# Two transformer blocks on one core: the MLP in four parts, the embedding's product shared between two norms

## The chip, the cores and the metric

The program runs on one core of one Trainium2 chip. The metric is the device time of one execution in microseconds, median of several runs. The core's engines are TensorE (matmuls; PE in the profile), VectorE (DVE), ScalarE (ACT), GpSimd (POOL) and SyncE (SP), whose queue issues the loads of weights.

## The reference

A first block (a gated delta rule mixer, then sliding-window attention) and a second block over 512 tokens of width 1024. The change touches the second block from the mixer's output product on, of which this is the code:

```python
mix = jnp.concatenate([y_pool, y_sb], axis=-1) @ w_out[i]
h = h + rms_norm_2(mix, g_mix_post[i])

m = rms_norm_2(h, g_mlp_pre[i]) @ w_up[i]          # 1024 -> 4096
m = jnp.square(jax.nn.relu(m)) @ w_down[i]         # 4096 -> 1024
h = h + rms_norm_2(m, g_mlp_post[i])

gate = jax.nn.sigmoid(h @ w_ple_gate[i])           # 1024 -> 1024
e = rms_norm_2(p[i] @ w_ple_proj[i], g_ple[i])     # 256 -> 1024
h = h + gate * e
```

All of it is in float32.

## The kernel before

**Layout.** Activations lie transposed: channels on the 128 partitions, the 512 tokens along the free axis, so a tensor of width 1024 is eight tiles of 128x512. A product's output of 128 channels is a "group", made in one of the PSUM banks.

**Products.** Each float32 operand is split in a high and a low part, and a product of one 128x128 piece of weights is three matmuls (high x high, high x low, low x high), made by `mm3` through line L736. One such triple is a "step". Weights come in blocks of eight pieces (128x1024, 512 KB). SyncE loads a block into one of four raw buffers, ScalarE makes its high part (L1223), VectorE its low part (L1819); `Pace` says at which point of the program each block is split: two blocks ahead as a rule (`open`), or a burst (`ahead`). `block_order` lists the blocks in the order of use.

**Order.** Every engine has a program of its own, and all follow one common script, `follow`. `gemm` is a generator whose `walk` yields the events OPEN, MM, LATE, CLOSE and STEP. With `wide` = 3 the first three groups go side by side, a piece of each in turn, so that a product can start while its inputs still arrive. CLOSE is where VectorE and ScalarE drain a group. `take(g, n)` advances a generator by n steps, `do` runs a named part of each engine that has one. Six banks (`WIDE`) are used in rotation.

**Norms.** The squares of eight tiles (ScalarE, `square`) are added up on VectorE (`accumulate`; L2214 for the first, L2217 for the others) into `sqa`; `rstd` sums over partitions by two float32 matmuls with a matrix of ones (`sqa`, and the last square in `sqt`), and ScalarE takes Ln (L1533) and Exp (L1547) into `rb`.

**Around the change.** After the mix product `rstd(3)` gives the factor and `post(0)` runs through eight pieces: VectorE scales the drained `mo` (L2418), the residual is added into `h` (piece 0 on VectorE, L2422, pieces 1 to 7 on GpSimd, L2583), ScalarE writes the high part of the next product's input `xm` (L1764), VectorE the low part (L2411; L2409 in `post(1)`). The semaphore `hv` stands for piece 0, `h[2]` and `h[3]` for the others. The squares of the new `h` are made and added behind that (`stats_h`), with 21 steps of the up product in between, and then `rstd(4)`.

The MLP goes in two halves of the inner width, each an up product of 16 groups and a down product of eight groups of 16 pieces. An up group is drained by relu times factor (VectorE, L1971, into `sqt`), square (ScalarE, L1275), high part (ScalarE, L1279) and low part (VectorE, L1974) into `xr`. The first down product is drained by ScalarE (L1289), the second by an add on VectorE (L1982). `begin_p` loads and splits the embedding's input between the halves.

Behind the MLP stands `ple`, the embedding's product: eight groups of two steps, each drained twice by ScalarE (L1788 a copy, L1793 a square into `pf`) and followed by a matmul of that square with the ones matrix. `rstd(5)` stands after the fourth. `post(1)` then feeds the gate product, `rstd(6)` scales the embedding (L2228), and each gate group ends with sigmoid (L1296), a product and an add (L1990, L1995) and its store.

Of the kernel before, what the change touches and what calls it, by code (L numbers as in the profile page):

```python
# [63 lines left out]

def block_order():
# [70 lines left out]
def walk(groups, wide=0, skew=0):  # L136
# [4 lines left out]
    if wide:  # L141
# [10 lines left out]
        for n in range(wide):  # L152
            yield CLOSE, n, groups[n][-1]
            yield STEP,
    for n in range(wide, len(groups)):
        blocks = groups[n]
        for at, i in enumerate(blocks):
            yield OPEN, n, i, at == 0
            for kk in range(8):
                k = 8 * at + kk  # L160
                yield MM, n, i, kk, k, k == 0, k == 8 * len(blocks) - 1
                yield STEP,
        yield CLOSE, n, blocks[-1]
        yield STEP,
# [63 lines left out]
def weave(g, order, parts, beside):  # L228
# [8 lines left out]
    for name in parts:  # L237
# [12 lines left out]
         "stick0": 12, "stick1": 14, "ple": 8}  # L250
# [10 lines left out]
def follow(p):  # L261
# [137 lines left out]
    for _ in range(3):  # L399
        next(up)  # L400
    drain(up)
    for half in range(2):
        if half:
            drain(gemm("up", single_groups("wu", 16, 16), 0, 1))
            do("begin_p")
        drain(gemm("down", [[("wd", 16 * half + 2 * n), ("wd", 16 * half + 2 * n + 1)] for n in range(8)], 0, half))

    ple = part("ple")
    for _ in range(4):
# [13 lines left out]
class Memory:  # L423
# [123 lines left out]

    def gain(self, key, i):
        return self.gcol[key][:, i:i + 1]
# [10 lines left out]
    def pieces(self, key):  # L560
# [4 lines left out]
        if key in ("ao", "bo", "down"):  # L565
            return [(x[:, k, :], x[:, 16 + k, :]) for k in range(16)]
# [7 lines left out]
class Signals:  # L574


    def __init__(self, nc, ctx):
        def new(name):
# [34 lines left out]
        self.h, self.hv = [new(f"h{n}") for n in range(4)], new("h_first_piece")  # L613
# [25 lines left out]
        self.d0, self.d1 = new("down_first"), new("down_second")  # L639
        self.phi, self.plo = new("p_hi"), new("p_lo")  # L640
        self.pe_p, self.pe_e, self.pe_s, self.pe_sum, self.pe_v = (
            new(n) for n in ("ple_pe", "ple_kept", "ple_sq", "ple_sum", "ple_scaled"))
# [80 lines left out]
def tensor_program(e, m, s):  # L723
# [24 lines left out]
    def await_piece(name, k, a):  # L748
# [18 lines left out]
        elif name == "down":  # L767
            e.wait_ge(s.hidlo, 16 * a + k + 1)
# [3 lines left out]
    def drained(name, n, a):  # L772
# [18 lines left out]
        if name == "up":  # L791
            return [(s.relu, 16 * a + n + 1)]
        if name == "down":
            return [((s.d0, s.d1)[a], n + 1)]
# [3 lines left out]
    def gemm(name, groups, wide=0, a=None, skew=0):  # L798
        X, bank = m.pieces(name), {}
        for what, *at in walk(groups, wide, skew):  # L800
# [178 lines left out]
    def rstd(r):  # L979
        if r == 6:  # L980
            return
# [191 lines left out]
    def ple():  # L1173
        def total(f):
            if f == 0:
                cleared(3)
            e.wait_ge(s.pe_s, f + 1)
            mm(m.banks[3][:], m.ones, m.pf[:, f % 2, :], f == 0, f == 7).then_inc(s.pe_sum, 1)

        for f in range(8):  # L1180
            half, n = f // 4, f % 4
            i = BLOCK["wp", half]
            wh = m.wh[:, i % N_SPLIT, :].rearrange("p (n k m) -> p n k m", n=4, k=2)
            wl = m.wl[:, i % N_SPLIT, :].rearrange("p (n k m) -> p n k m", n=4, k=2)
            b = ring.next()
            cleared(b)
            if n == 0:
                e.wait_ge(s.wlo, i + 1)
            if f == 0:
                e.wait_ge(s.plo, 2)  # L1190
            for k in range(2):
                ins = mm3(m.banks[b][:], wh[:, n, k, :], wl[:, n, k, :], m.xp[:, k, :], m.xp[:, 2 + k, :], k == 0, k == 1)
            ins.then_inc(s.wused if n == 3 else s.pe_p, 1)
            clear[b] = [(s.pe_e, f + 1), (s.pe_s, f + 1)]
            if f:
                total(f - 1)
            yield
        total(7)
# [4 lines left out]
def scalar_program(e, m, s):  # L1203
# [22 lines left out]
    def gemm(name, groups, wide=0, a=None, skew=0):  # L1226
        bank = {}
        for what, *at in walk(groups, wide, skew):
# [42 lines left out]
    def evac_up(n, bank, i, half):  # L1271
        f = m.sqt[:, n % 2, :]
        at = 16 * half + n + 1
# [3 lines left out]
        if n == 0:  # L1277
            e.wait_ge(s.wused, (BLOCK["wd", 15] if half else BLOCK["wco", 7]) + 1)
        e.activation(m.XR[:, n, :], f, ACT.Copy).then_inc(s.hidhi, 1)  # L1279

    def evac_down(n, bank, i, half):
        if half:
            square(4, n)
            return
        e.wait_ge(s.wused, i + 1)
        if n == 0:
            e.wait_ge(s.hv, 1)
            e.wait_ge(s.h[2], 7)
        e.activation(m.mo[:, n, :], bank[:], ACT.Copy).then_inc(s.d0, 1)  # L1289

    def evac_gate(n, bank, i, a):
        e.wait_ge(s.wused, i + 1)
        if n == 0:
            e.wait_ge(s.hv, 2)
            e.wait_ge(s.h[3], 7)
# [205 lines left out]
    def square(r, n, tile=None):  # L1501
# [15 lines left out]
        elif r == 3 and n == 0:  # L1517
            e.wait_ge(s.hv, 1)
        elif r == 3:
            e.wait_ge(s.h[2], n)  # L1520
        elif r == 4:
            e.wait_ge(s.d1, n + 1)
# [5 lines left out]
    def rstd(r):  # L1528
        if r == 6:
            e.wait_ge(s.pe_sum, 8)  # L1530
# [225 lines left out]
    def post(at):  # L1756
        for n in range(8):
            if n == 0:
                e.wait_ge(s.hv, at + 1)
                e.wait_ge(s.wused, (BLOCK["wd", 31] if at else BLOCK["wco", 7]) + 1)  # L1760
            else:
                e.wait_ge(s.h[2 + at], n)
            scale = 1.0 if at else m.gain("g_mlp_pre", n)
            e.activation(m.xm[:, n, :], m.H[:, n, :], ACT.Copy, scale=scale).then_inc(s.shi, 1)  # L1764
            if n == 1:
                split(pace.ahead(4))
# [8 lines left out]
    def ple():  # L1775
# [1049 lines left out]
```

## Time and profile before

| | us |
|---|---|
| runs | 1678.0, 1679.5, 1684.57; median 1679.5 |
| profiled execution | 1678.48, its span in the profile 1676.7 |
| TensorE busy | 1580.9 (94%), mean granted clock 0.984 |
| VectorE busy | 865.4 (52%) |
| ScalarE busy | 745.0 (44%) |
| GpSimd busy | 264.9 (16%) |
| chain that ended last | 79% TensorE, 8% VectorE, 7% ScalarE |

The span runs from the first instruction to the last; the profiled execution's own time has 1.8 us around it. Busy shares are means over all stages. The granted clock is TensorE's, as a share of full speed (2.4 GHz); its lower level, 0.50, is 1.2 GHz.

### The profile page before, as it was taken

How to read it: one execution, taken by the hardware profiler on the slowest of the kernel's cores; microseconds unless marked ns; L12 is line 12 of the kernel's file. 1: busy time of each engine (PE TensorE's matmuls, PEld its weight loads, DVE VectorE, ACT ScalarE, POOL GpSimd, SP SyncE). 2: the span in 40 equal slices, each digit the busy share in tenths (PEclk: the TensorE clock that was granted, in tenths of full speed). 3: DMA queues.
4: the chain of work that ended last, by engine and by line, in shares of the span. 5: the costliest groups of instructions: out<-in, count | busy, mean ns of one | idle time of the engine just before them, and what ended most of it. 6: DMA issues, size and time to landing. Idle time of an engine off the chain costs nothing.

```text
span 1676.7 us, 20632 instructions
## 1 busy us (share of the span) xinstructions
PE 1580.9 (94%) x7700; PEld 1238.5 (74%) x7700; DVE 865.4 (52%) x1596; ACT 745.0 (44%) x1293; POOL 264.9 (16%) x465
## 2 busy tenths in 40 slices
PE   7789999998889999999998999999989999999988
PEld 5577888887777876777775787666667888888866
DVE  4667666766654455555555435444365422444346
ACT  4443454345443255656666323555535322343243
POOL 1033324332222000322222200000020000000010
PEclk9799999999999999999999999999989999999999
DMA  4121211111113323122221132111122233222321
GB/s 176 63 76 39 63 64 63 54 50 44 45 51 105 101 90 113 64 76 74 72 76 60 61 100 83 53 56 49 50 70 88 95 106 101 88 90 99 101 75 51
DMA packets 40163, 127.22 MB, mean 76 GB/s; under 512 B 4576, under 2 KB 9104, under 8 KB 40064
## 3 DMA queue, kind: packets, MB, share of 16 engines
q1 hardware_dynamic: 38112, 121.65, 22.3%
q0 software_dynamic: 1040, 3.27, 0.6%
q8 instruction: 62, 1.02, 0.2%
q10 hardware_dynamic: 912, 0.99, 0.2%
q14 instruction: 37, 0.30, 0.1%
HBM read 122.69 MB, written 2.15 MB: 74 GB/s over the span
## 4 chain that ended last, share of the span: by engine, by line
PE 79%; DVE 8%; ACT 7%; issue 3%; POOL 2%; DMA 1%; SPq 0%; ACTq 0%; DVEq 0%; POOLq 0%
PE ps L736 77%; ACT L L1627 3%; DVE wl L1819 2%; DVE L L2295 1%; PE ps L1065 1%; PE ps L861 1%; ACT wh L1223 1%; POOL h L2583 1%; DVE qkv L1855 1%; DMA wraw<-in_wa 1%; DVE qb L1904 1%; POOL L L2568 1%; ACT L L1579 0%; DVE mo L2418 0%; DVE U L2148 0%
## 5 line engine op out<-in xcount | busy, mean ns | idle before, releaser
L736 PE MATMUL ps<-xr,wh 128*128 128x512 f32 x2752 | 902.2, 409 | 17.7 <-DVE wl L1819 15.3
L736 PEld LDWEIGHTS ps<-xr,wh 128*128 128x128 f32 x2752 | 504.7, 190 | 145.9 <-issue 40.8
L736 PE MATMUL ps<-xr,wl 128*128 128x512 f32 x1376 | 543.2, 395 | 0.0
L1819 DVE TENSOR_TENSOR wl<-wraw,wh 128x1024 fp32r<-128x1024 f32 x214 | 261.1, 1233 | 181.9 <-ACT wh L1223 180.6
L736 PEld LDWEIGHTS ps<-xr,wl 128*128 128x128 f32 x1376 | 261.0, 190 | 57.7
L1223 ACT ACTIVATE wh<-wraw 128x1024 fp32r<-128x1024 f32 x214 | 220.6, 1048 | 34.1 <-PE ps L736 30.4
L736 PE MATMUL ps<-xm,wh 128*128 128x512 f32 x640 | 202.5, 398 | 11.4 <-DVE xm L2411 7.1
L736 PEld LDWEIGHTS ps<-xm,wh 128*128 128x128 f32 x640 | 121.5, 191 | 42.5 <-issue 9.4
L2568 POOL TENSOR_SCALAR L<-L,m 128x256 f32<-128x256 f32 (+1 forms) x128 | 80.7, 655 | 313.8 <-DVE m L2310 313.8
L736 PE MATMUL ps<-xm,wl 128*128 128x512 f32 x320 | 126.1, 394 | 0.0
L2583 POOL TENSOR_TENSOR h<-h,mo 128x512 f32<-128x512 f32 x14 | 20.5, 1462 | 598.0 <-DVE mo L2418 598.0
L1855 DVE SCALAR_TENSOR_TENSOR qkv<-cin,gains,qkv 128x512 f32<-128x512 f32 x96 | 73.7, 769 | 4.0 <-ACT qkv L1251 3.0
L1627 ACT ACTIVATE L<-L,m 128x256 f32<-128x256 f32 (+1 forms) x128 | 59.9, 469 | 28.3 <-DVE m L2301 28.3
L736 PEld LDWEIGHTS ps<-xm,wl 128*128 128x128 f32 x320 | 61.2, 191 | 13.1
L1275 ACT ACTIVATE sqt<-sqt 128x512 f32<-128x512 f32 x32 | 20.2, 632 | 92.8 <-DVE sqt L1971 92.8
L2295 DVE CUSTOM_DVE_ANT_0 L<-ps,bias,sinks 128x256 f32<-128x256 f32 (+1 forms) x128 | 51.1, 443 | 19.8 <-PE ps L736 19.8
L1525 ACT ACTIVATE sqt<-h 128x512 f32<-128x512 f32 x24 | 15.0, 630 | 101.1 <-DVE h L1884 54.6
L2536 POOL TENSOR_TENSOR masks<-nb,uc 128x60 f32<-128x60 f32 (+14 forms) x120 | 45.0, 375 | 79.1 <-DVE nb L2115 63.0
L1251 ACT ACTIVATE qkv<-cin,gains 128x512 f32<-128x512 f32 x32 | 23.0, 722 | 66.2 <-DVE cin L1869 66.2
L1647 ACT ACTIVATE pT<-ps 128x512 f32<-128x512 f32 x32 | 19.2, 599 | 71.9 <-PE ps L1065 71.8
L2538 POOL TENSOR_TENSOR uc<-uc,masks 128x60 f32<-128x60 f32 (+14 forms) x120 | 43.4, 362 | 9.4
L1974 DVE TENSOR_TENSOR xr<-sqt,xr 128x512 fp32r<-128x512 f32 x32 | 22.2, 692 | 43.6 <-ACT xr L1279 43.6
(257 smaller groups left out, 1801.5 us busy)
## 6 DMA issues: line engine op xcount, KB each, us to landing
wraw<-in_wa SPq DMA_DIRECT2D x48, 512.0 KB, 3.8
wraw<-in_wb SPq DMA_DIRECT2D x32, 512.0 KB, 3.8
wraw<-in_wu SPq DMA_DIRECT2D x32, 512.0 KB, 3.7
wraw<-in_wd SPq DMA_DIRECT2D x32, 512.0 KB, 3.7
wraw<-in_wao SPq DMA_DIRECT2D x16, 512.0 KB, 3.7
wraw<-in_wbo SPq DMA_DIRECT2D x16, 512.0 KB, 3.8
wraw<-in_wc SPq DMA_DIRECT2D x16, 512.0 KB, 3.7
bias<-rel_rows SPq DMA_DIRECT2D x16, 256.0 KB, 4.0
```

The lines of the kernel that those rows point to most:

```text
L736: return e.matmul(out, w, x, start=start, stop=stop, skip_group_check=True)
L1223: e.activation(m.wh[:, i % N_SPLIT, :], m.raw[:, i % N_RAW, :], ACT.Copy).then_inc(s.whi, 1)
L1251: e.activation(m.qkv[:, h % 2, n, :], m.cin[:, b, 3:515], ACT.Copy, scale=m.convw[:, 3, ch:ch + 1]).then_inc(s.conv0, 1)
L1627: e.activation(x, x, ACT.Exp, bias=m.nmx[:, c, u:u + 1], accum_out=m.den[:, c, u:u + 1]).then_inc(s.ex, 1)
L1819: e.tensor_tensor(m.wl[:, i % N_SPLIT, :], m.raw[:, i % N_RAW, :], m.wh[:, i % N_SPLIT, :].bitcast(F), ALU.subtract).then_inc(s.wlo, 1)
L1855: e.scalar_tensor_tensor(out=dst, in0=m.cin[:, c % 2, w:w + 512], scalar=m.convw[:, w, ch:ch + 1], in1=dst, op0=ALU.mult, op1=ALU.add).the ...
L1974: e.tensor_tensor(m.XR[:, 16 + n, :], f, m.XR[:, n, :].bitcast(F), ALU.subtract).then_inc(s.hidlo, 1)
L2295: e.tensor_tensor_reduce(out=m.L[:, c, ee, n, lo:], in0=m.banks[4 + ee][:, 256 * (n % 2) + lo:256 * (n % 2) + 256], in1=m.bias[:, c, ee, lo:],
L2536: did(e.tensor_tensor(part, nb[:, :, r + 1:], m.uc[:, :, r:r + 1].to_broadcast([128, 4, w]), ALU.mult))
L2538: did(e.tensor_tensor(m.uc[:, :, r + 1:], m.uc[:, :, r + 1:], part, ALU.add))
L2568: e.tensor_scalar(x, x, m.den[:, c, 2 * n + ee:2 * n + ee + 1], 1.0, ALU.mult, ALU.mult).then_inc(s.pr, 1)
L2583: e.tensor_tensor(m.H[:, n, :], m.H[:, n, :], m.mo[:, n, :], ALU.add).then_inc(s.h[2 + at], 1)
```

## The change

- The MLP goes in four parts of 1024 inner channels: up of eight groups, down of eight groups of eight pieces, four times. The first down product is drained by ScalarE, the other three are added to it by VectorE. The hidden tiles' low parts are made one group later than before, behind the next group's relu, and `up_end` makes the last.
- The embedding's product is cut in two halves of four groups; one half stands at the norm after the mix (one step of it ahead of `rstd(3)`, seven behind), the other at the norm after the MLP. The blocks `wp` move accordingly in the order of weights, and `begin_p` moves into the mix product.
- The squares of the embedding are no longer summed by eight matmuls: ScalarE squares the kept tiles later (four behind the first up product, four in the gate product), VectorE adds them up, and one matmul with the ones matrix remains.
- All residual adds are on VectorE, each followed by the next piece's scaling; GpSimd's `post` is gone.
- In the up product of part 0 and in the gate product the three wide groups start one piece apart (`skew` = 1) and two more groups are made before any is drained (`hold` = 2). The sums of the squares of `h` are added in behind the 24 wide steps, and `rstd(4)` and `rstd(6)` stand ten steps into the held groups.

```diff
+def up_groups(a):
+    return [[("wu", 8 * a + n)] for n in range(8)]
+def down_groups(a):
+    return [[("wd", 16 * (a // 2) + 2 * n + a % 2)] for n in range(8)]
...
-    for half in range(2):
-        out += [("wu", 16 * half + b) for b in range(16)]
-        out += [("wd", 16 * half + b) for b in range(16)]
-    out += [("wp", b) for b in range(2)]
+    out += [("wp", 0)]
+    for a in range(4):
+        out += [b for g in up_groups(a) + down_groups(a) for b in g]
+    out += [("wp", 1)]
...
-def walk(groups, wide=0, skew=0):
+def walk(groups, wide=0, skew=0, hold=0):
...
         yield LATE,
-        for n in range(wide):
-            yield CLOSE, n, groups[n][-1]
-            yield STEP,
+    done = list(range(wide))
     for n in range(wide, len(groups)):
+        if done and n == wide + hold:
+            yield from close(groups, done)
+            done = []
...
-        yield CLOSE, n, blocks[-1]
+        done.append(n)
+        if n >= wide + hold:
+            yield from close(groups, done)
+            done = []
+    yield from close(groups, done)
...
+    drain(take(mix, 24))
+    do("begin_p")
     drain(mix)
-    do("rstd", 3)
-    do("post", 0)
-    up = gemm("up", single_groups("wu", 16), 3, 0)
-    for n in range(8):
-        do("stats_h", n)
-        for _ in range(3 if n < 7 else 0):
-            next(up)
-    do("rstd", 4)
...
+    def normed(r, at):
+        ple = part("ple", at)
+        post = part("post", at)
         next(ple)
-    do("rstd", 5)
-    drain(ple)
-    do("post", 1)
-    gate = gemm("gate", single_groups("wg", 8), 3)
+        do("rstd", r)
+        drain(take(ple, 3))
+        for _ in range(2):
+            next(post)
+            drain(take(ple, 2))
+        drain(ple)
+        drain(post)
+
+    normed(3, 0)
+    for a in range(4):
+        up = gemm("up", up_groups(a), *((0, a) if a else (3, a, 1, 2)))
+        if a == 0:
+            drain(take(up, 24))
+            for n in range(8):
+                if n == 4:
+                    next(up)
+                do("stats_h", n)
+            drain(take(up, 9))
+            do("rstd", 4)
+        drain(up)
+        do("up_end", a)
+        if a == 0:
+            for f in range(4):
+                do("square_e", f)
+        drain(gemm("down", down_groups(a), 0, a))
+
+    normed(5, 1)
+    gate = gemm("gate", single_groups("wg", 8), 3, None, 1, 2)
+    drain(take(gate, 24))
+    for f in range(4, 8):
+        do("square_e", f)
+    drain(take(gate, 9))
     do("rstd", 6)
     drain(gate)
...
     def rstd(r):
         if r == 6:
+            cleared(3)
+            e.wait_ge(s.pe_acc, 7)
+            mm(m.banks[3][:], m.ones, m.esum).then_inc(s.pe_sum, 1)
             return
...
-            if f:
-                total(f - 1)
-            yield
-        total(7)
...
+    def square_e(f):
+        e.wait_ge(s.pe_e, f + 1)
+        if f >= 3:
+            e.wait_ge(s.pe_acc, f - 2)
+        elif f:
+            e.wait_ge(s.plo, 2)
+        e.activation(m.pf[:, f % 2, :] if f else m.esum, m.e[:, f, :], ACT.Square).then_inc(s.pe_s, 1)
...
+        if n:
+            hid_low(n - 1, a)
+    def hid_low(n, a):
+        e.wait_ge(s.hidhi, 8 * a + n + 1)
+        e.tensor_tensor(m.XR[:, 8 + n, :], m.sqt[:, n % 2, :], m.XR[:, n, :].bitcast(F),
+                        ALU.subtract).then_inc(s.hidlo, 1)
...
-        e.tensor_tensor(m.mo[:, n, :], bank[:], m.mo[:, n, :], ALU.add).then_inc(s.d1, 1)
-        accumulate(4, n)
+        e.wait_ge(s.down[a - 1], n + 1)
+        e.tensor_tensor(m.mo[:, n, :], bank[:], m.mo[:, n, :], ALU.add).then_inc(s.down[a], 1)
+        if a == 3:
+            accumulate(4, n)
...
+        scaled(0)
+        for n in range(8):
+            e.wait_ge(s.post, 8 * at + n + 1)
+            e.tensor_tensor(m.H[:, n, :], m.H[:, n, :], m.mo[:, n, :], ALU.add).then_inc(s.h[2 + at], 1)
+            if n < 7:
+                scaled(n + 1)
+            low(n)
+            if n in (1, 5):
+                split(pace.ahead(3 if n == 1 else 4))
+            yield
...
-    def post(at):
-        for n in range(1, 8):
-            e.wait_ge(s.post, 8 * at + n + 1)
-            e.tensor_tensor(m.H[:, n, :], m.H[:, n, :], m.mo[:, n, :], ALU.add).then_inc(s.h[2 + at], 1)
```

## Rows read from the trace of the kernel before

**Rows 1.** The page, busy time of TensorE: us, share of the span, instructions.
```profile
PE 1580.9 (94%) x7700; PEld 1238.5 (74%) x7700; DVE 865.4 (52%) x1596; ACT 745.0 (44%) x1293; POOL 264.9 (16%) x465
```

**Rows 2.** TensorE's waits, 1180 to the end: releaser, us in total, times, longest.
```profile
PE ps L736 <- DVE xm L2411: 7.1, 4, 5.6
PE ps L736 <- DVE xm L2409: 3.9, 5, 1.4
PE ps L736 <- DVE sqa L2217: 3.8, 1, 3.8
```

**Rows 3.** The drains of the first down half: duration min/median/max, first and last start.
```profile
L1289 ACT ACTIVATE mo<-ps x8: 598/598/598, 1351.3 to 1427.4; 128x512 f32<-128x512 f32 x8
```

**Rows 4.** Timeline of TensorE, first norm: start, us, instruction, [idle before, releaser].
```profile
1232.80 1.12 PE L736 MATMUL ps<-sqt,k 128*128 128x512 f32 x2
...
1239.52 0.77 PE L736 MATMUL ps<-xm,wh 128*128 128x512 f32 x1 [5.60 <-DVE xm L2411]
...
1263.97 1.10 PE L736 MATMUL ps<-sqa,k 128*128 128x512 f32 x2 [3.84 <-DVE sqa L2217]
```

**Rows 5.** Timelines of VectorE and of ScalarE, first norm.
```profile
1235.34 0.75 DVE L2418 SCALAR_TENSOR_TENSOR mo<-mo,gains,rb 128x512 f32<-128x512 f32 x1 [5.35 <-ACT rb L1547]
1236.12 0.69 DVE L2422 TENSOR_TENSOR h<-h,mo 128x512 f32<-128x512 f32 x1
...
1249.08 1.78 DVE L2418 SCALAR_TENSOR_TENSOR mo<-mo,gains,rb 128x512 f32<-128x512 f32 x1
...
1254.02 1.77 DVE L2418 SCALAR_TENSOR_TENSOR mo<-mo,gains,rb 128x512 f32<-128x512 f32 x1
...
1259.15 4.67 DVE L2217 TENSOR_TENSOR sqa<-sqa,sqt 128x512 f32<-128x512 f32 x6
...
1238.86 0.72 ACT L1764 ACTIVATE xm<-h,gains 128x512 fp32r<-128x512 f32 x1 [1.29 <-POOL h L2583]
```

**Rows 6.** Timeline of GpSimd, first norm.
```profile
1248.57 1.74 POOL L2583 TENSOR_TENSOR h<-h,mo 128x512 f32<-128x512 f32 x1 [1.29 <-DVE mo L2418]
```

**Rows 7.** Windows: length, busy of PE, PEld, DVE, ACT, POOL, granted clock, DMA share, GB/s.
```profile
120.00:124.00 4.00, 1.18 (x8) 0.78 (x8) 0.00 (x0) 3.34 (x5) 0.00 (x0) 1.00 0.01 2
484.00:488.00 4.00, 2.00 (x10) 1.78 (x11) 3.59 (x5) 4.00 (x8) 1.23 (x1) 0.86 0.00 0
1240.00:1248.00 8.00, 7.39 (x18) 5.20 (x17) 7.20 (x7) 2.88 (x4) 2.99 (x2) 0.50 0.39 131
1480.00:1520.00 40.00, 40.00 (x178) 33.10 (x178) 20.35 (x25) 17.49 (x24) 0.00 (x0) 1.00 0.28 92
```

**Rows 8.** Timeline of TensorE, second norm: sums by the ones matrix.
```profile
1609.55 1.02 PE L736 MATMUL ps<-pf,k 128*128 128x512 f32 x2
1610.41 1.02 PE L736 MATMUL ps<-sqa,k 128*128 128x512 f32 x2
```

**Rows 9.** Timelines of VectorE and ScalarE, second norm.
```profile
1601.51 0.69 DVE L1982 TENSOR_TENSOR mo<-ps,mo 128x512 f32<-128x512 f32 x1 [6.12 <-PE ps L736]
...
1602.29 0.63 ACT L1525 ACTIVATE sqt<-mo 128x512 f32<-128x512 f32 x1 [8.35 <-DVE mo L1982]
...
1640.70 0.69 DVE L2409 TENSOR_TENSOR xm<-h,xm 128x512 fp32r<-128x512 f32 x1
```

**Rows 10.** Timelines of VectorE and of ScalarE, gate product.
```profile
1642.01 5.39 DVE L2228 SCALAR_TENSOR_TENSOR xreg<-xreg,gains,rb 128x512 f32<-128x512 f32 x8 [0.62 <-ACT rb L1547]
1647.32 1.22 DVE L1819 TENSOR_TENSOR wl<-wraw,wh 128x1024 fp32r<-128x1024 f32 x1
1648.45 0.69 DVE L1990 TENSOR_TENSOR mo<-mo,xreg 128x512 f32<-128x512 f32 x1
...
1649.78 0.68 DVE L1990 TENSOR_TENSOR mo<-mo,xreg 128x512 f32<-128x512 f32 x1
...
1643.72 1.06 ACT L1223 ACTIVATE wh<-wraw 128x1024 fp32r<-128x1024 f32 x1 [1.81 <-PE ps L736]
...
1672.22 0.60 ACT L1296 ACTIVATE mo<-ps 128x512 f32<-128x512 f32 x1 [4.84 <-PE ps L736]
```

More of the change, by code:

```diff
@@ L791, in drained, with gemm @@
         if name == "up":
-            return [(s.relu, 16 * a + n + 1)]
+            return [(s.relu, 8 * a + n + 1)]
         if name == "down":
-            return [((s.d0, s.d1)[a], n + 1)]
+            return [(s.down[a], n + 1)]
         return [(s.gs, n + 1)]
     @part
-    def gemm(name, groups, wide=0, a=None, skew=0):
+    def gemm(name, groups, wide=0, a=None, skew=0, hold=0):
         X, bank = m.pieces(name), {}
-        for what, *at in walk(groups, wide, skew):
+        for what, *at in walk(groups, wide, skew, hold):
             if what == OPEN:
@@ L1225, in gemm @@
     @part
-    def gemm(name, groups, wide=0, a=None, skew=0):
+    def gemm(name, groups, wide=0, a=None, skew=0, hold=0):
         bank = {}
-        for what, *at in walk(groups, wide, skew):
+        for what, *at in walk(groups, wide, skew, hold):
             if what == OPEN:
@@ L1774, in ple @@
     @part
-    def ple():
-        for f in range(8):
-            half, n = f // 4, f % 4
+    def ple(half):
+        split(pace.open())
+        for n in range(4):
+            f = 4 * half + n
             b = ring.next()
-            if n == 0:
-                split(pace.open())
-                if half == 0:
-                    e.wait_ge(s.wused, BLOCK["wd", 31] + 1)
+            yield
             if n == 3:
@@ L1822, in gemm @@
     @part
-    def gemm(name, groups, wide=0, a=None, skew=0):
+    def gemm(name, groups, wide=0, a=None, skew=0, hold=0):
         bank = {}
-        for what, *at in walk(groups, wide, skew):
+        for what, *at in walk(groups, wide, skew, hold):
             if what == OPEN:
@@ L2435, in ple, with square_e @@
     @part
-    def ple():
-        for f in range(8):
+    def ple(half):
+        split(pace.open())
+        for n in range(4):
             ring.next()
-            if f % 4 == 0:
-                split(pace.open())
-            if f % 4 == 3:
-                pace.finish()
             yield
+            yield
+        pace.finish()
+    @part
+    def square_e(f):
+        if f:
+            e.wait_ge(s.pe_s, f + 1)
+            if f > 1:
+                e.wait_ge(s.pe_acc, f - 1)
+            e.tensor_tensor(m.esum, m.esum, m.pf[:, f % 2, :], ALU.add).then_inc(s.pe_acc, 1)
     follow(p)
@@ L2455, in gemm @@
     @part
-    def gemm(name, groups, wide=0, a=None, skew=0):
-        for what, *_ in walk(groups, wide, skew):
+    def gemm(name, groups, wide=0, a=None, skew=0, hold=0):
+        for what, *_ in walk(groups, wide, skew, hold):
             if what == STEP:
@@ L2616, in gemm @@
     @part
-    def gemm(name, groups, wide=0, a=None, skew=0):
-        for what, *at in walk(groups, wide, skew):
+    def gemm(name, groups, wide=0, a=None, skew=0, hold=0):
+        for what, *at in walk(groups, wide, skew, hold):
             if what == OPEN:
@@ L2673, in post, with ple @@
     def post(at):
-        split(pace.ahead(4))
+        for n in range(8):
+            if n in (1, 5):
+                split(pace.ahead(3 if n == 1 else 4))
+            yield
     @part
-    def ple():
-        for f in range(8):
-            if f % 4 == 0:
-                split(pace.open())
-            if f % 4 == 3:
-                pace.finish()
-            yield
+    def ple(half):
+        split(pace.open())
+        yield from idle(8)
+        pace.finish()
     @part
```

143 lines of the change are left out of this document (56 added, 87 removed).

## The prediction

> **What bounds it now.** The page comes first: TensorE is busy for 94% of the span [rows 1], so time can only come out of its gaps, its slow stretches, or work taken from it. Next I read its waits over the part that the diff touches, from the mix product to the end [rows 2]: 14.8 us, all of it beside the two norms that feed the up product (7.1 and 3.8) and the gate product (3.9); inside the MLP there is none. Then its speed where nothing holds it: the eight drains of the first down half start over 76.1 us, 16 steps of three matmuls apart, so a step (one 128x128 piece of weights, high and low parts) costs 76.1 / 7 / 16 = 0.68 us [rows 3]. Then, engine by engine, the norms.
>
> First norm. Statistics end, Ln and Exp follow, VectorE scales, adds, and feeds piece by piece [rows 5]. TensorE stands 5.60 us before its first up piece and 3.84 us before the second statistics, for which VectorE makes its adds only after the last piece [rows 4, 6]. The granted clock is 0.50 from 1240 to 1248, the lower of its two levels [rows 7]. From the second statistics 491 of the MLP's 512 steps are left; at 0.68 (0.6795 unrounded) they take 333.6 us, and TensorE starts them at 1265.7 and ends at 1601.5: another 2.2 us lost to the clock. The pieces come slowly because GpSimd adds seven of eight residual pieces: beside one of its 1.74 us adds VectorE's scaling takes 1.78 us in place of 0.75 [rows 5, 6].
>
> Second norm. The embedding's eight products (two steps each) run first, each with a sum by the 128x128 ones matrix: such a sum takes 0.86 us (start to start) [rows 8]. The last gate piece is written from 1640.70 on, 39.2 us behind the last down drain at 1601.51 [rows 9].
>
> **The change, part by part.** All in time of the trace of before.
>
> Statistics to first scaling. Before the statistics' two sums TensorE now runs one embedding step, 0.68 us. From the second sum's start to the first scaling it was 1235.34 - 1232.80 = 2.54 us, and stays so; hence s, the start of the first scaling, is 1235.34 + 0.68 = 1236.02. ScalarE's weight split (1.05 [rows 10]) for the embedding's opening falls into the time before that sum ends. The other seven steps (4.8 us) run from 1234.3 to 1239.1, under the chain.
>
> Pieces, on VectorE alone. Per piece: add 0.69, ScalarE's pass 0.72, the low part, and in the shadow of that pass the next scaling. With 0.02 us from engine to engine and a scaling's pitch of (5.39 - 0.75) / 7 = 0.66 [rows 10], the period is 0.69 + 0.02 + 0.72 + 0.02 + 0.66 = 2.11 us; in the second norm, with ScalarE at 0.63 and a subtraction of pitch 0.61 [rows 9, 10], 1.97. In before, scalings two pieces apart start 4.94 us apart (1249.08, 1254.02), 2.47 a piece [rows 5]. The first low part starts at s + 0.78 + 1.45 = s + 2.23 (second norm s + 2.14). Two weight splits stand in the row: each waits for ScalarE's 1.05 and takes 1.13, less 0.66 overlapped, 1.5 us each. The last low part is done at s + 2.23 + 14.8 + 3.0 + 0.75 = s + 20.8 = 1256.8. The first is done at 1239.0, as TensorE ends the embedding: the 5.6 us gap goes.
>
> Skew and hold. The three wide groups start one piece apart, and two more follow before any is drained, so from the last piece TensorE has 6 + 10 = 16 steps, 10.9 us, to 1267.7. The next statistics (4.67 us for six adds [rows 5], the copy, two or three weight splits of 1.2) end about 7 us behind the last piece, near 1264: the 3.84 goes. Two sums, 1.72, and 512 - 34 = 478 steps, 324.8 us, follow: the last down group ends at **1594.2**, against 1601.5. First term: **7.3 us**.
>
> MLP in four parts. The count of matmuls stays. VectorE gets 16 more drains of 0.69, ScalarE none; VectorE was busy about half the time in the MLP's busiest window (20.35 of 40 us [rows 7]), so nothing. New are three more handovers from up to down. The first down group needs the last hidden tile only at its eighth step, 4.8 us in; that tile's chain is relu 0.69, square 0.63, copy 0.63, subtraction 0.69 and hops, 2.8 us: 2 us to spare. Five held tiles leave behind the norm's factor; with relu of the next tile ahead of this one's subtraction both engines need about 1.4 a tile, 7 us, and the sixth group has a free bank, the seventh the first drained: no wait. The embedding's squares (0.6) and adds (0.72) stand behind the last hidden tile and ahead of a split wanted two groups (10.9 us) later: hidden. The input p and its split move from the MLP into the mix product; its DMA, behind y on GpSimd's queue, lands before ScalarE asks, and on SyncE's queue one block of the embedding's weights only takes the place of another block of the same size: nothing.
>
> Second norm, counted from the old 1601.5. One step to 1602.2, first sum to 1603.0; the square of the last down tile ends at 1602.92 [rows 9], in time. Second sum from 1603.0, s = 1605.6; embedding done at 1608.6. The last piece is done at s + 2.14 + 13.8 + 3.0 + 0.69 = s + 19.6 = 1625.2. 46 steps are left, 31.3 us, and one sum, 0.86: TensorE ends at 1657.4. In before it ends at 1672.2, where the last sigmoid starts [rows 10]. Second term: **14.8 us**; 6.0 of it is the seven sums of 0.86 that VectorE and ScalarE now make between other work. One place is tight. Counted from the start of the sum for the embedding, its factor is there after 2.5 us (sum, Ln, Exp); VectorE then scales eight tiles (5.31), drains five held groups (1.33 each [rows 10]: 6.65) and splits the last weights (1.2): 15.8 with hops. TensorE wants these weights after the sum's 0.86, six steps and two groups of eight (15.0): 15.8 too. 0 to 0.5 us, taken as 0.1. The sum itself is a new wait of TensorE, with group five of the gate queued behind it; its last term is added near 1628, and TensorE gets there at 1625.2 + 10.9 = 1636.1.
>
> The clock. In the skewed start TensorE has one step for the first piece and two for the second, and the first split delays the third: gaps of 1.3 and 2.2 us, 1.4 us of work in 5. What follows is not in the trace of before. Nearest rows: with 1.18 us of work in 4 the clock stayed at 1.00 (120 to 124); with 2.00 in 4 it fell (0.86 from 484 on); behind 5.60 and 3.84 us of standing it fell [rows 4, 7]. The one stretch at the lower level lasted 8.5 us (1239.5 to 1248), the other, from the 2.2 us it lost, about 4.4. Below it costs nothing; above, 8.5 us at half speed lose 4.3, less 1.5 of gaps that hold it: 2.8 in each norm, 5.6 in all. I take 1.5, one fall in two norms. The Trainium skill, "TensorE: Matmul & The Clock Gate", section "A second HAM failure mode: psum-queue depth-cycling", says that short idling between groups of matmuls can make the clock swing between its levels; by that rule both norms would see it, which is rival (a). The row of 120 to 124 speaks against it here, that of 484 for it.
>
> Sum: 7.3 + 14.8 - 0.1 - 1.5 = 20.5 us. The profiled execution took 1678.5, so 1658.0; it lies 1.0 below the median of the runs, 1679.5. Forecast **1659**.
>
> **Rivals.**
> (a) The clock falls in both norms and stays low for as long as the longest stretch: 4.1 beyond what I took, 1663. For: gaps of 1.3 to 2.2 in both. Against: six steps in a row come behind them.
> (b) VectorE's row is no faster than before, because scaling and add do not overlap behind each other's signals: the period stays near 2.47. 7 x (0.36 + 0.50) = 6.0 us: 1665. For: three operations and two handovers in each piece. Against: VectorE's long times stand only beside GpSimd [rows 5, 6].
> (c) Handovers wait: the last two hidden tiles go through one behind the other and behind a split, 2 x 2.75 + 1.2 = 6.7 against 4.8 at four places: 7.7 us, 1667. Against: both engines are idle most of an up group.
> (d) The other side: the thinner start keeps TensorE at half clock. A step costs 0.55 us more there (7.39 us for 18 matmuls [rows 7], 1.23 against 0.68). It decides from (22.0 + 3) / 0.55 = 46 steps on; if all 24 wide and 10 held steps of both norms run so, 68 steps cost 37 less 3 us of gaps: 1657.5 + 34 = 1692. Against: no row shows more than 8.5 us of it.
> (e) The change does not do what it says only if the chain through the norms was not the limit; the waits name its members one by one [rows 2].
>
> **How the numbers follow.** Forecast case 0.62, (a) 0.14, (b) 0.11, (c) 0.07, (d) 0.03, something cheaper than every bound (no fall at all, smaller hops) 0.03. The forecast case alone runs from 1655.5 (no clock loss, hops 1 us less) to 1662. With (a) and most of (b) the range is 1654.5 to 1665.5; outside are (c), (d) and the rest. A difference of 0.5% (8.4 us) is about what a measurement can tell: all but (d) are faster than 1671.
>
> **What would show it.** No idle of TensorE over 2.5 us in either norm; first scaling near 1236.0, last low part of the first norm near 1256.8; period 2.1; the second statistics waited for by nobody; last down tile near 1594; one ones-sum before the gate's factor; from there to the last piece 24 us. A third piece that starts at clock 0.50, a TensorE wait on the hidden low part (the eighth step of a down group), or on the weights of the last gate group would show it wrong.

## The result

The changed kernel takes 1660.5 us (median of 4 runs, 1657.0 to 1662.2) against 1681.1 for the kernel before (4 runs, one more than the three known at the forecast): ratio 0.9874, 95% interval 0.9847 to 0.9902. Forecast were 1659 and a range of 1654.5 to 1665.5. The profiled execution took 1661.3, its span 1659.5.

The spans differ by 17.2 us, less than the 20.5 I had worked out, but not where the diff is. I compare one stretch, from the start of ScalarE's last square of the mix product to the start of the last gate sigmoid, cut at the start of the last down drain on VectorE:

| us | mix to last down drain | to the last sigmoid | stretch |
|---|---|---|---|
| before | 369.4 | 70.7 | 440.1 |
| changed | 362.8 | 56.5 | 419.3 |
| difference | 6.6 | 14.3 | **20.8** |
| predicted (7.3 and 14.8, less 1.6) | | | 20.5 |

The stretch begins at 1232.1 before and at 1235.7 in the changed kernel, though the change leaves what stands ahead of it, but for `begin_p` in the mix product, as it was. The mean granted clock of the spans, 0.984 and 0.981, makes 53 and 63 us at the lower level, of which the stretch itself has 13.7 and 3.4. Of the 3.6 us, 2.9 arise between 620 and 666 us, where only the changed kernel's trace has a fall (6.8 us, from 641 on); where the clock falls there differs from execution to execution. All experiments below are therefore read from the stretch of their one profile first, and from their runs second. A part of the stretch that an edit leaves alone comes out the same to 0.1 us, except where the clock differs inside it (0.3 us in the second part of e6, 0.85 in the first of e8).

TensorE's waits from 1180 on, changed kernel (who was waited for, us in total, times, longest):

```profile
PE ps L776 <- DVE xm L2445: 3.7, 3, 1.8
PE ps L776 <- DVE xm L2447: 3.0, 2, 1.9
PE ps L776 <- ACT am L1755: 1.1, 1, 1.1
```

They answer to [rows 2]: 14.8 us have become 6.7 (L2447 is the low part of the first norm, L2445 that of the second). The wait for the statistics (`sqa`) has gone. For the rest an estimate from these traces: waits for the embedding's squares and for a block of weights (1.5 us) are gone too, seven sums of 0.86 are gone (6.0), and TensorE works 3.4 us at the lower clock and not 11.3, which at half speed is 3.9. With the 8.1 us of waits that makes 19.5 of the 20.8.

Timeline of TensorE in the first norm, changed kernel (start, us, instruction, idle before it), against [rows 4]:

```profile
1237.06 1.02 PE L776 MATMUL ps<-sqt,k 128*128 128x512 f32 x2
...
1244.78 0.73 PE L776 MATMUL ps<-xm,wh 128*128 128x512 f32 x2 [1.12 <-DVE xm L2447]
...
1248.35 0.85 PE L776 MATMUL ps<-xm,wh 128*128 128x512 f32 x2 [1.91 <-DVE xm L2447]
...
1271.52 1.02 PE L776 MATMUL ps<-sqa,k 128*128 128x512 f32 x2
```

The second statistics start with no idle time ahead of them. The longest gap is 1.9 us where it was 5.6. VectorE, the same norm, against [rows 5]:

```profile
1239.50 0.75 DVE L2454 SCALAR_TENSOR_TENSOR mo<-mo,gains,rb 128x512 f32<-128x512 f32 x1 [0.51 <-ACT rb L1575]
1240.29 0.69 DVE L2460 TENSOR_TENSOR h<-h,mo 128x512 f32<-128x512 f32 x1
...
1248.21 0.68 DVE L2460 TENSOR_TENSOR h<-h,mo 128x512 f32<-128x512 f32 x1
...
1250.35 0.69 DVE L2460 TENSOR_TENSOR h<-h,mo 128x512 f32<-128x512 f32 x1
...
1254.93 1.23 DVE L1848 TENSOR_TENSOR wl<-wraw,wh 128x1024 fp32r<-128x1024 f32 x1 [0.20 <-ACT wh L1255]
...
1259.69 0.75 DVE L2447 SCALAR_TENSOR_TENSOR xm<-h,gains,xm 128x512 fp32r<-128x512 f32 x1 [0.79 <-ACT xm L1790]
```

From one residual add to the next 2.14 us (2.11 predicted); the first scaling starts 2.44 us behind the second sum (2.54), the last low part ends 20.94 behind the first scaling (20.8). The granted clock there (windows; columns as in [rows 7]):

```profile
1246.00:1248.00 2.00, 0.44 (x2) 0.01 (x1) 1.87 (x4) 0.72 (x1) 0.00 (x0) 1.00 0.40 84
1248.00:1250.00 2.00, 1.65 (x5) 1.31 (x6) 1.88 (x4) 0.72 (x1) 0.00 (x0) 0.70 0.44 178
1250.00:1252.00 2.00, 2.00 (x7) 1.51 (x6) 1.87 (x4) 0.73 (x1) 0.00 (x0) 0.50 0.00 0
1252.00:1254.00 2.00, 2.00 (x10) 1.66 (x9) 1.87 (x4) 0.78 (x2) 0.00 (x0) 0.95 0.00 0
```

Behind the gap it fell to 0.50 (1.2 GHz), for 3.4 us. It happened in one norm of two. The Trainium skill, "TensorE: Matmul & The Clock Gate", section "A second HAM failure mode: psum-queue depth-cycling", describes a clock that swings between its levels where TensorE idles shortly and often between groups of matmuls; here the trace agrees in the first norm (one fall, behind gaps of 1.1 and 1.9 us) and not in the second (none, behind 0.9 and 1.8).

The second norm on VectorE, and the first piece on ScalarE, against [rows 8 to 10]:

```profile
1598.53 0.69 DVE L2018 TENSOR_TENSOR mo<-ps,mo 128x512 f32<-128x512 f32 x1 [1.81 <-PE ps L776]
...
1602.55 0.75 DVE L2454 SCALAR_TENSOR_TENSOR mo<-mo,gains,rb 128x512 f32<-128x512 f32 x1 [0.40 <-ACT rb L1575]
...
1621.70 0.69 DVE L2445 TENSOR_TENSOR xm<-h,xm 128x512 fp32r<-128x512 f32 x1 [0.70 <-ACT xm L1790]
...
1635.35 5.39 DVE L2264 SCALAR_TENSOR_TENSOR xreg<-xreg,gains,rb 128x512 f32<-128x512 f32 x8 [6.06 <-ACT rb L1575]
...
1647.50 1.22 DVE L1848 TENSOR_TENSOR wl<-wraw,wh 128x1024 fp32r<-128x1024 f32 x1
...
1604.12 0.63 ACT L1790 ACTIVATE xm<-h 128x512 fp32r<-128x512 f32 x1 [0.29 <-DVE h L2460]
```

The first piece of the kernel before, where the last down drain starts at 1601.51:

```profile
1621.42 1.15 ACT L1764 ACTIVATE xm<-h 128x512 fp32r<-128x512 f32 x2
```

So ScalarE writes the first piece 5.6 us behind the last down drain, 19.9 before, and that is 14.3 us, as much as the whole second part gained. Behind it the last piece comes another 1.7 us sooner, and 1.8 us more follow the last piece.

TensorE, the late factor's sum by the ones matrix (`k`), inside the fifth gate group, with no idle time ahead of it (33 gate steps come before it, nine of them of the held groups and not ten; ahead of `rstd(4)` it is 34 up steps):

```profile
1632.84 1.02 PE L776 MATMUL ps<-xreg,k 128*128 128x512 f32 x2
```

The low part of the last piece starts 23.2 us behind the last down drain, 39.2 before. The last gate weights are ready at 1648.7, and TensorE does not wait for them.

### The profile page after: what moved, and what is told of

Read it like the earlier page. It is cut to its first block, busy times and chain, and to the rows that moved or that the text cites. A ratio compares the mean times of both kernels' runs of the same rounds, so it can differ in the third digit from the quotient of the medians.

```text
span 1659.5 us, 20679 instructions
## 1 busy us (share of the span) xinstructions
PE 1578.6 (95%) x7686; PEld 1240.5 (75%) x7686; DVE 875.4 (53%) x1633; ACT 746.9 (45%) x1293; POOL 244.3 (15%) x451
## 4 chain that ended last, share of the span: by engine, by line
PE 81%; DVE 7%; ACT 7%; issue 3%; POOL 1%; DMA 1%; SPq 0%; ACTq 0%; DVEq 0%; POOLq 0%
PE ps L776 79%; ACT L L1655 3%; DVE wl L1848 2%; DVE L L2331 1%; PE ps L1108 1%; PE ps L901 1%; ACT wh L1255 1%; DVE qkv L1884 1%; DMA wraw<-in_wa 1%; DVE qb L1933 1%; POOL L L2614 1%; ACT L L1607 0%; DVE h L2460 0%; DVE U L2184 0%; ACT xm L1790 0%
## 5 line engine op out<-in xcount | busy, mean ns | idle before, releaser
L2018 DVE TENSOR_TENSOR mo<-ps,mo 128x512 f32<-128x512 f32 x24 | 16.6, 692 | 66.9 <-PE ps L776 66.9
L1999 DVE SCALAR_TENSOR_TENSOR sqt<-ps,rb 128x512 f32<-128x512 f32 x32 | 22.0, 691 | 41.0 <-PE ps L776 36.0
```

Of the source, the lines that this page charges most:

```text
L1999: e.scalar_tensor_tensor(out=m.sqt[:, n % 2, :], in0=bank[:], scalar=0.0, in1=m.rb[:], op0=ALU.max, op1=ALU.mult).then_inc(s.relu, 1)
```

## The experiments

Columns: stretch and its two parts in us, from one profile; ratio of the runs to the kernel before with its 95% interval. The changed kernel stands in the first line. Each ratio is to runs of the kernel before made beside that version (their medians are 1680.2 to 1684.3), so ratios can be compared and medians only roughly. The expectations of e1 to e4 cut the stretch slightly differently (419.5 and 440.3 us for what is 419.3 and 440.1 here).

| | first part | second part | stretch | median of runs | ratio |
|---|---|---|---|---|---|
| changed | 362.8 | 56.5 | 419.3 | 1660.5 | 0.9874 (0.9847 to 0.9902) |
| e1 adds on GpSimd | 364.8 | 59.2 | 423.9 | 1662.8 | 0.9899 (0.9879 to 0.9919) |
| e2 no skew | 361.1 | 54.5 | 415.6 | 1656.0 | 0.9854 (0.9827 to 0.9881) |
| e3 sums back | 363.4 | 57.2 | 420.6 | 1660.6 | 0.9889 (0.9872 to 0.9906) |
| e5 embedding whole | 362.2 | 64.0 | 426.2 | 1667.2 | 0.9906 (0.9888 to 0.9923) |
| e10 the same, split in time | 362.4 | 58.0 | 420.4 | 1662.1 | 0.9875 (0.9857 to 0.9894) |
| e6 factor first | 363.9 | 56.8 | 420.7 | 1659.8 | 0.9862 (0.9845 to 0.9878) |
| e7 row cleared | 357.9 | 51.9 | 409.8 | 1648.5 | 0.9794 (0.9774 to 0.9814) |
| e11 e7, sums back | 360.7 | 55.4 | 416.1 | 1656.9 | 0.9847 (0.9828 to 0.9866) |
| before | 369.4 | 70.7 | 440.1 | 1681.1 | 1 |
| e4 before, four parts | 369.4 | 70.7 | 440.0 | 1683.6 | 1.0024 (1.0012 to 1.0035) |
| e8 before, one sum | 370.2 | 64.4 | 434.6 | 1676.7 | 0.9955 (0.9937 to 0.9973) |
| e9 before, adds on VectorE | 366.8 | 67.8 | 434.6 | 1676.2 | 0.9962 (0.9945 to 0.9978) |

**e1, the residual adds back on GpSimd** (changed kernel).

```diff
+            if n == 0:
                 e.tensor_tensor(m.H[:, n, :], m.H[:, n, :], m.mo[:, n, :], ALU.add).then_inc(s.h[2 + at], 1)
...
+    def post(at):                                   # GpSimd
+        for n in range(8):
+            if n:
+                e.wait_ge(s.h[2 + at], n)
+                e.wait_ge(s.post, 8 * at + n + 1)
+                e.tensor_tensor(m.H[:, n, :], m.H[:, n, :], m.mo[:, n, :], ALU.add).then_inc(s.h[2 + at], 1)
+            yield
```

> The changed kernel with residual adds 1 to 7 of both norms back on GpSimd. Stretch measured: end of the mix product to the start of the last gate sigmoid, 419.5 us in the changed kernel, 440.3 before. Theory (VectorE's row of add, scaling and low part sets the time to the last piece; GpSimd's adds slow it): a piece takes 2.47 again in place of 2.15 and 2.00, so 7 x 0.32 + 7 x 0.47 = 5.5 us more, 425. Rival (GpSimd takes work off VectorE and the add is hidden under ScalarE's pass): no change or less, 418 to 420.

Measured 423.9, 4.6 more against the theory's 5.5; the rival falls. VectorE, then GpSimd, in this run:

```profile
1246.18 0.74 DVE L2447 SCALAR_TENSOR_TENSOR xm<-h,gains,xm 128x512 fp32r<-128x512 f32 x1
1246.85 1.77 DVE L2454 SCALAR_TENSOR_TENSOR mo<-mo,gains,rb 128x512 f32<-128x512 f32 x1
1248.87 1.74 DVE L2447 SCALAR_TENSOR_TENSOR xm<-h,gains,xm 128x512 fp32r<-128x512 f32 x1 [0.24 <-ACT xm L1790]
...
1246.40 1.67 POOL L2632 TENSOR_TENSOR h<-h,mo 128x512 f32<-128x512 f32 x1 [1.35 <-DVE mo L2454]
```

The long operations of 1.77 and 1.74 us are back exactly beside GpSimd's adds. From the last low part to the last down drain it took 338.1 us, as in the changed kernel, and here the clock did not fall in the first norm: behind the last piece nothing is left of the changed kernel's fall.

**e2, no skew** (changed kernel): `(3, a, 1, 2)` becomes `(3, a, 0, 2)`, and the gate's skew 0 too.

> The changed kernel with skew 0 in the up product of part 0 and in the gate product (hold stays 2). Theory (the last piece's time is set by VectorE's row and TensorE keeps up with three steps of 2.04 us a piece in either order, so what counts is how many steps are left at the last piece): 43 in place of 46 steps, 2.0 us less in each norm, 415.4 us for the stretch of 419.5. Rival (the skew is what fills the start and brings part of the gain): 2 to 6 us more, as TensorE waits for the third block's weights and then has all three groups to catch up.

Measured 415.6: the theory to 0.2 us. The last low parts come at the same places (they end 24.7 behind the start of the stretch and 23.9 behind the down drain, as in the changed kernel), and three steps fewer are left. TensorE's waits from 1200 on show what the start looks like now, one wait of up to 1.9 us in each norm on the third block's weights:

```profile
PE ps L776 <- DVE wl L1848: 3.7, 2, 1.9
PE ps L776 <- DVE xm L2445: 0.2, 1, 0.2
```

**e3, eight sums back** (changed kernel): `mm(m.banks[3][:], m.ones, m.k1[:, 0:512])` behind each group of `ple`.

> The changed kernel with eight more matmuls by the ones matrix (0.86 us each), one behind each group of the embedding, four in each norm; their moving operand is a constant tile and their result is not used. Theory as in the prediction's second term (a sum removed is 0.86 us of TensorE's path): 6.9 us more, 426.4. Rival (in the new order TensorE stands 3.0 and 3.7 us in these places anyway, so the sums would have been nearly free; only ScalarE's copies and with them the first pieces come later): 0 to 2.5 us more.

Measured 1.3 more, not 6.9: the rival. The sums fill what were gaps: over both norms TensorE waits 2.8 us for pieces in place of 6.7, the longest wait 1.2. What they cost comes with later pieces: ScalarE writes the second norm's first piece 0.5 us later, and VectorE's last low part ends 0.6 and 0.7 us later. That ScalarE's copies of the embedding, which wait for later groups, are what delays them is read from the order of its work.

**e4, four parts alone** (kernel before). Its order of blocks, parts, semaphores and drains as in the change, but the hidden tile's low part at once:

```diff
-    for half in range(2):
-        if half:
-            drain(gemm("up", single_groups("wu", 16, 16), 0, 1))
-            do("begin_p")
-        drain(gemm("down", [[("wd", 16 * half + 2 * n), ("wd", 16 * half + 2 * n + 1)] for n in range(8)], 0, half))
+    for a in range(4):
+        if a:
+            drain(gemm("up", up_groups(a), 0, a))
+        if a == 2:
+            do("begin_p")
+        drain(gemm("down", down_groups(a), 0, a))
```

> The kernel before with nothing but the MLP in four parts (its order of blocks, eight-piece down products, 16 more adds on VectorE). Stretch in the kernel before 440.3 us. Theory (each handover from up to down has 2 us to spare and the adds lie beside TensorE's work): 440.3, within 1 us. Rival (the last hidden tiles come late at four places): 7.7 us more, 448.

The stretch is the same to 0.1 us, and the waits are those of [rows 2]:

```profile
PE ps L746 <- DVE xm L2422: 7.1, 4, 5.6
PE ps L746 <- DVE xm L2420: 3.8, 5, 1.4
PE ps L746 <- DVE sqa L2228: 3.8, 1, 3.8
```

Over its runs this kernel was 0.24% (4 us) slower all the same. Its profiled execution was the fastest of its ten and has 1.9 us ahead of the stretch, in stages that it does not touch; where the rest comes from was not found, so for the stretch of this one execution the four parts cost nothing, and for the whole program that is not shown.

**e5 and e10, the embedding whole at the second norm** (changed kernel). Nothing of it at the first norm; at the second its 16 steps go before and between the pieces, its eight squares behind the gate's wide steps.

```diff
     def normed(r, at):
         post = part("post", at)
+        if not at:
+            do("rstd", r)
+            drain(post)
+            return
+        ple = chain(part("ple", 0), part("ple", 1))
         next(ple)
         do("rstd", r)
         drain(take(ple, 3))
-        for _ in range(2):
+        for _ in range(6):
             next(post)
             drain(take(ple, 2))
```

> The changed kernel with the embedding's product whole at the second norm again (no half at the first; its 16 steps stand between the sums and the gate product, its eight squares behind the gate's wide steps). Stretch in the changed kernel 419.3 us: 362.8 to the last down drain, 56.5 from there. Theory (TensorE has idle places in both norms, so moving eight steps costs little on either side): the factor of the first norm comes 0.6 earlier, but TensorE stands over 5 us and the clock falls longer than now, 362 to 365 for the first part; in the second the 16 steps end 4.6 us later than the eight, and TensorE catches up with the pieces but for about 1 us, 57.5. In all 420 to 422.5. Rival (the half was 5.4 us taken off the second norm's path): 424.7 or more.

Measured 426.2, which looks like the rival. But the first part, 362.2, is the theory's, and in the second (64.0 against 57.5) TensorE waited for weights:

```profile
PE ps L776 <- DVE xm L2447: 5.7, 3, 4.6
PE ps L776 <- DVE wl L1848: 3.8, 1, 3.8
```

The block of the third gate group needs the buffer of the first embedding block, and my point for its split came too late; the clock fell there as well (6.8 us). The run doesn't separate the two. e10 adds a split point at piece 3:

```diff
-            if n in (1, 5):
-                split(pace.ahead(3 if n == 1 else 4))
+            if n in (1, 5) or (n == 3 and at):
+                split(pace.ahead(4 if n == 5 else 3))
```

> As the run with the embedding whole at the second norm, but the weights of the third gate group are split two pieces earlier, so that TensorE does not wait 3.8 us for them. Theory: 362.2 to the last down drain; from there the 16 steps end 12.6 us behind it, the 24 wide ones at 28.9, and 40 steps and a sum follow: 57 to 58, in all 419 to 420.5, so that moving the half is worth about nothing against the 419.3 of the changed kernel. Rival (the half is 5.4 us off the path): 424.7.

Measured 420.4 (362.4 and 58.0), on the theory: the half at the first norm is worth 1.1 us, not 5.4, in a second norm whose TensorE had idle places. And with the whole embedding in it the first piece is still written 5.6 us behind the last down drain.

**e6, the factor ahead of the held groups** (changed kernel).

```diff
             for n in range(8):
-                if n == 4:
-                    next(up)
                 do("stats_h", n)
-            drain(take(up, 9))
             do("rstd", 4)
```

> The changed kernel with the statistics of the up product summed straight behind the 24 wide steps and not ten steps later. Theory: the adds end 5.4 us behind the last piece, TensorE is there 4.1 us behind it, so it stands 1.3 us: 420.6 for the stretch of 419.3. Rival (the late place is what removed the 3.84 us wait of before, so that wait comes back): 423.1, and the clock falls with it.

Measured 420.7, on the theory in all but not in its parts: 1.05 us more lie in the first part, where the edit is, and 0.3 in the second, which it leaves alone and where the clock fell in this run. TensorE waits 0.8 us for the sum of squares:

```profile
PE ps L773 <- DVE sqa L2250: 0.8, 1, 0.8
```

So with the sum ahead of the ten held steps 0.8 of the old 3.84 us is still there, and its late place is worth 1.05 us. (The two held groups are still made here; a kernel without them was not tried.) The adds' move to VectorE accounts for 0.7 of the other 3.0: in e9 this wait is 3.2. That the rest went because the sums now follow the row in one run, with 24 steps ahead of them, is my reading of the code.

This run also shows what a fall of the clock in the row costs. In its first norm the clock stayed at 1.00, and its last low part ends 24.7 us behind the start of the stretch, as in the changed kernel with its fall. TensorE stood once more instead, 1.25 us, before the seventh piece:

```profile
1255.22 0.73 PE L773 MATMUL ps<-xm,wh 128*128 128x512 f32 x2 [1.25 <-DVE xm L2444]
...
1241.00:1261.00 20.00, 16.19 (x67) 12.13 (x68) 17.65 (x26) 10.24 (x16) 0.00 (x0) 1.00 0.16 53
1610.40:1613.80 3.40, 3.40 (x9) 2.63 (x8) 3.37 (x6) 0.96 (x2) 0.00 (x0) 0.50 0.00 0
```

The last line is its second norm, with the fall that the changed kernel does not have there: the last low part comes at the same place (23.9), and 0.3 us are lost behind it.

**e7, the row cleared** (changed kernel), built on what e2 showed. Skew 0; one more block is split at the last mix and down groups and at the embedding's opening; no split in `post`; and the next block is split behind the wide steps:

```diff
-    def open(self):
+    def open(self, more=0):
...
-        return self.upto(min(i + 1 + LEAD, min(self.finished, i) + N_SPLIT))
+        more = more or (ORDER[i] in (("wco", 7), ("wd", 31)))
+        return self.upto(min(i + 1 + LEAD + more, min(self.finished, i) + N_SPLIT))
...
     def ple(half):
-        split(pace.open())
+        split(pace.open(1))
...
-            if n in (1, 5):
-                split(pace.ahead(3 if n == 1 else 4))
...
+    def more():
+        split(pace.ahead(1))
```

> The changed kernel with skew 0 and with the two weight splits taken out of VectorE's row of pieces: one is made ahead of the first scaling, one behind the last piece. Against the run without skew (stretch 415.6). Theory (the row sets the last piece; each split in it costs 1.5 us): the last piece 3 us earlier, from where TensorE itself is nearly the limit: 410 to 411. Rival (the splits only move to where the statistics and the factor wait for them): 413 to 416.

Measured 409.8, just under the theory. The row from the first scaling to the last low part takes 18.1 and 16.9 us in place of 20.9 and 19.8, and that is the 5.8 us by which the stretch is shorter than in e2. From 1200 on TensorE waits 0.2 us in all. 1648.5 us in the runs; by the ratios 0.8% below the changed kernel, and their intervals do not touch: the fastest version here.

**e11, e7 with the eight sums of e3.**

> The run with the cleared row (stretch 409.8) with the eight extra sums of the earlier run, which cost 1.3 us in the changed kernel. Theory (a sum costs what TensorE's idle places do not hold; with the row cleared there are none): 8 x 0.86 = 6.9 more, 416 to 417. Rival (they stay nearly free behind the chain of the factor): 411 to 412.

Measured 6.3 more than e7, against 1.3 in e3: the same sums, at nearly their full 6.9 once TensorE has no idle place.

**e8, the kernel before with one sum of eight.** The call of `total(f - 1)` in `ple` is left out, so the embedding's norm takes the last square alone; ScalarE, which waited for a sum before it wrote `pf` again, waits for its own square there.

> The kernel before with seven of the eight sums of the embedding's squares left out (the one left takes the last square alone, so the embedding's norm is not the reference's). From the last down drain to the last sigmoid it was 70.7 us. Theory (what counts is what delays the factor, and behind it VectorE's row; of the seven sums three stand ahead of the factor, with the stall of TensorE on the first square): 3 to 3.7 us less, 67.0 to 67.7. Rival, the accounting in the prediction (each sum is 0.86 us of TensorE's path): 6.0 less, 64.7.

Measured 64.4 in the second part, 6.3 less: my theory here was wrong and the prediction's accounting right. The factor did come only 3.6 us sooner, as I expected, but the first piece 6.3: ScalarE writes it 13.6 us behind the last down drain (1606.90) and not 19.9. ScalarE in this run:

```profile
1619.56 0.60 ACT L1785 ACTIVATE xreg<-ps 128x512 f32<-128x512 f32 x1 [0.27 <-PE ps L736]
1620.05 0.59 ACT L1790 ACTIVATE pf<-ps 128x512 f32<-128x512 f32 x1
1620.53 1.16 ACT L1761 ACTIVATE xm<-h 128x512 fp32r<-128x512 f32 x2
```

In this order ScalarE drains and squares the last embedding group before it may write the first piece, so every sum that holds TensorE back holds the first piece back, even where the factor is there.

**e9, the kernel before with the adds on VectorE**, in the changed kernel's order of scaling, add and low part; GpSimd's `post` is gone.

> The kernel before with nothing changed but the residual adds, all on VectorE in the changed kernel's order of scaling, add and low part. Stretch before: 369.4 to the last down drain, 70.7 from there. Theory (a piece takes 2.15 and 2.00 us in place of 2.47 and 2.44): 2.3 less in the first norm, 2.2 to 3.1 less in the second, 434.5 to 436 in all. Rival (adds on VectorE alone give nothing, since the statistics and ScalarE's squares set the ends): 439 to 441.

Measured 434.6 (2.5 less in the first part, 2.9 in the second): the theory.

## Why the prediction was right

- **Statistics to first scaling**: 2.44 and, in the second norm, 2.55 us from the second sum, predicted 2.54. Right.
- **Pieces on VectorE**: 2.14 us a piece against 2.11, last piece at 20.94 against 20.8; second norm 19.84 against 19.6. e9 gives the step alone, 5.5 us; e1, which undoes it, 4.6.
- **Skew and hold**: the 16 steps behind the last piece were counted rightly (10.9 us, measured 11.1), and what I did not see is that three of them are the skew's own price. e2: 3.7 us in all. That the sum stands ten steps late is worth 1.05 (e6); the hold itself was not taken out.
- **First term**: 7.3 predicted, 6.6 measured. The last piece came within 0.1 of its place behind the start of the stretch (24.7). From there to the down drain it took 338.1, worked out as 337.4: 0.2 of that lies ahead of the sums, 0.5 in the 478 steps behind them, 0.6805 us each and not 0.6795. The prediction's 2.2 us "lost to the clock" in the kernel before has the same 0.5 in it: at the lower level TensorE worked 3.4 us there, a loss of 1.7.
- **Four parts**: nothing, as predicted. e4 shows it within the stretch; the handovers cost nothing, and no row of the changed kernel shows a wait on a hidden tile.
- **Second term**: 14.8 predicted, 14.3 measured; the last piece 0.2 late and TensorE 0.4 behind it. Its sentence that 6.0 of it is the seven sums holds for the kernel before (e8: 6.3) and not for the changed one: put back there, eight cost 1.3 (e3). The price was right in one order and wrong in the other. What the sum does not name is that all of this term lies ahead of the first piece (19.9 us behind the last down drain, now 5.6). e8 takes 6.3 of these 14.3 away with the sums, and e10 shows that it isn't the half moved to the first norm; the other 8 go with the order, the norm's two sums behind one embedding step and not behind four groups, and the first piece ahead of the embedding's last steps. That order alone was not tried.
- **The clock**: one fall in two norms, as taken, but for 3.4 us and not the 8.5 that it was priced by (the trace of before has falls of 10.2 and 3.4 us), and its price was 0 and not 1.5. The row was the limit while it lasted: the changed kernel with the fall and e6 without it have the last low part at the same place, and e1 without it takes the same 338.1 behind that. The sign of being wrong that I had named, a third piece at 0.50, was missed by little: it started at 1248.35, and the clock fell at 1248.8.
- **The sum**: 20.5 against 20.8 is closer than its terms are. The two terms came out 1.3 us too large, and 1.6 us were taken off for a fall and a wait that cost nothing; that these errors nearly cancel is luck.
- **Rivals**: (a) did not come; with the clock low for longer (e10: 10.2 us in the first norm) the first part was still 362.4. (b) falls to e9 and e1, (c) to e4, (d) to the clock's 3.4 us.

The gain is not a sum of parts. Alone on the kernel before, adds give 5.5, sums about 6, four parts 0. Taken out of the changed kernel alone, adds cost 4.6, sums 1.3, the embedding's half 1.1, the late place of the first norm's sum 1.05, and the skew gives 3.7 back. In e10, without any embedding at the first norm, the first part is 7.0 us shorter than before. About 2.5 of that is the adds (e9); the other 4.5 lie behind the last low part, where the wait of 3.84 us for the sum of squares and the fall of the clock behind it (1.7 us) are gone, and the skew's three steps take some of that back. The four parts free the tiles in which the kept embedding lies through the MLP; that this is their use was read from the code and not tried.

## What to carry to other kernels

Name the row of dependent work that sets the last input, then count what is left behind it: an edit is worth what it takes out of one of the two, and the same edit is worth little where the other engine stands idle (the same eight sums cost 1.3 us and 6.3 us). Housekeeping on the limiting engine's queue, as the weight splits here, costs its full time inside such a row (1.4 us for a split of 1.23) and nothing next to it: clearing two of them in each norm, and the skew, gave 9.5 us, nearly half as much as the whole change. Where executions differ by some microseconds in stages that are not touched, compare the stretch that is.

## What the runs showed of the hardware

- GpSimd's residual add of 1.67 us makes VectorE's operation beside it 1.77 in place of 0.75; it came back with the adds (e1) and went with them (e9).
- The granted clock fell behind a gap of 1.9 us in the changed kernel and not behind one of 1.8 in its second norm; in e6 it was the other way round, with the same two gaps (1.9 and 1.8), and in e1 it fell behind neither 1.9 nor 1.85. So the length of such a gap does not decide it here. At the lower level it lasted 3.4 us, and 10.2 from the end of the 4.6 us gap of e10 on, where 362.4 us for the first part show no loss either.
- A fall costs time where TensorE is the limit. In or right behind the old wait for the sum of squares (3.2 to 3.9 us) the clock fell in the kernel before, e4, e8 and e9, and not in e6, where that wait is 0.8. In e8 TensorE worked 5.1 us at the lower level there, in the kernel before 3.4, and the first part is 0.85 us longer: half of the 1.7.
- Ahead of the stretch, the same instructions took 1229.1 us (e1) to 1236.6 (e10), at mean clocks of the whole span of 0.991 and 0.981.
